# Joint attention: another order of the engines' work in a step, and the query blocks in natural order

## What is computed

```python
def _diff_combine(s, lam):
    p = jax.nn.softmax(s, axis=-1)
    ...
    return p[:, :, 0] - lam * p[:, :, 1]

def diff_attn_prompt(o, q, k, v, lam):      # 8 heads, blocks of 128 queries, causal
    ...
        s = jnp.einsum('bqhd,bkhd->bhqk', qi, k).astype(F32) * HD_C ** -0.5
        s = jnp.where((kpos[None, :] <= qpos[:, None])[None, None], s, -jnp.inf)
        a = _diff_combine(s, lam)
        return jnp.einsum('bhqk,bkhe->bqhe', a, vf)
...
def diff_attn_cached(q, k, v, kp, vp, lam): # 8 samples, 4096 cached keys each, in pages of 128
    s_p = jnp.einsum('bqhd,bkhd->bhqk', q, kp).astype(F32) * scale
    ...
```

## Time and profile before

| what | us |
|---|---|
| three executions | 2852.94, 2854.07, 3822.21 |
| their median | 2854.07 |
| the profiled execution: its own time | 2852.4 |
| its span, first to last instruction | 2850.3 |
| the 64 steps of `attend`, from the first block's scores to the end of the last step's key banks | 1931.9 to 2698.0 |
| busy over the whole span: PE, DVE, ACT | 2569.8, 1363.5, 780.2 |
| bytes moved by DMA | 536.54 MB |

### The profile page before, as it was taken

How to read it: one execution, slowest core, us unless ns; L and a number is a source line. 1 busy time by engine, 2 the same in 40 slices (tenths; PEclk the granted TensorE clock), 3 DMA queues, 4 the chain that set the end, 5 groups by cost and what they waited for, 6 DMA issues and landing times. The chain is left out here.

```text
span 2850.3 us, 46453 instructions
## 1 busy us (share of the span) xinstructions
PE 2569.8 (90%) x16842; PEld 1912.0 (67%) x16842; DVE 1363.5 (48%) x2338; ACT 780.2 (27%) x1978; POOL 416.2 (15%) x240
## 2 busy tenths in 40 slices
PE   6999999999946999499968999969999999999968
PEld 5898889888935777344437888855565566556547
DVE  3656562433242666312223343326766666667643
ACT  3222211111121333111111111114454455545521
POOL 4324321432200000000004232100000000000021
PEclk7999999999976999799989999988999999999979
DMA  4233222322217788732112525159999999999863
GB/s 125 91 105 97 80 84 93 118 71 84 77 41 210 236 269 278 215 146 83 48 55 70 143 84 142 55 160 345 353 384 368 363 359 383 371 354 374 294 203 117
DMA packets 332817, 536.54 MB, mean 188 GB/s; under 512 B 29765, under 2 KB 242130, under 8 KB 329402
## 3 DMA queue, kind: packets, MB, share of 16 engines
q1 hardware_dynamic: 329698, 525.33, 54.2%
q10 hardware_dynamic: 2936, 8.82, 0.8%
HBM read 432.73 MB, written 101.22 MB: 187 GB/s over the span
## 5 line engine op out<-in xcount | busy, mean ns | idle before, releaser
L2355 PE MATMUL at_ring<-ident,at_kp 128*128 128x128 f32 x2048 | 305.2, 281 | 25.3 <-ACT at_kT L2455 9.6
L2355 PEld LDWEIGHTS at_ring<-ident,at_kp 128*128 128x128 f32 x2048 | 225.0, 141 | 149.0 <-issue 117.8
L511 PE MATMUL p_col<-h_hi,p_wqk 128*128 128x352 f32 x768 | 250.5, 326 | 3.3 <-DVEq L713 3.3
L513 PE MATMUL p_col<-h_hi,p_wqk 128*128 128x352 f32 x768 | 246.6, 321 | 0.0
L512 PE MATMUL p_col<-h_lo,p_wqk 128*128 128x352 f32 x768 | 246.3, 321 | 0.0
L1657 PE MATMUL oa_out<-oa_w,oa_yT 128*128 128x512 f32 x512 | 225.8, 599 | 8.5 <-ACT oa_yT L1713 5.4
L2455 ACT ACTIVATE at_kT<-at_ring 128x512 f32<-128x512 f32 x256 | 153.4, 599 | 263.6 <-PE at_ring L2355 263.6
L1954 PE MATMUL p_gm<-p_whl,h_hi 128*128 128x512 f32 x512 | 202.3, 395 | 7.8 <-POOLq L2040 7.8
L2581 DVE COPY at_kT<-at_ring 128x512 f32<-128x512 f32 x256 | 176.9, 691 | 64.7 <-PE at_ring L2355 49.4
L555 PE MATMUL p_row<-p_wvz,h_hi 128*128 128x512 f32 x512 | 203.7, 398 | 3.3 <-ACT p_vst L632 3.3
L557 PE MATMUL p_row<-p_wvz,h_lo 128*128 128x512 f32 x512 | 202.0, 394 | 0.0
(11 more groups left out here) (368 smaller groups left out, 4436.1 us busy)
## 6 DMA issues: line engine op xcount, KB each, us to landing
at_kp<-in_cache_k SPq DMA_DIRECT2D x256, 512.0 KB, 5.9
at_vp<-in_cache_v SPq DMA_DIRECT2D x256, 512.0 KB, 5.9
s_qk<-p_res SPq DMA_DIRECT2D x32, 528.0 KB, 2.8
p_wst<-in_w_in_a SPq DMA_DIRECT2D x32, 512.0 KB, 4.0
p_wst<-in_w_in_a SPq DMA_DIRECT2D x64, 256.0 KB, 3.1
mx_qk<-s_qk SPq DMA_DIRECT2D x16, 1024.0 KB, 10.6
p_wst<-in_w_in_c SPq DMA_DIRECT2D x64, 256.0 KB, 5.6
s_v<-p_vst SPq DMA_DIRECT2D x64, 128.0 KB, 2.8
```

What stands on the lines that cost most here:

```text
L511: pe.matmul(out[:, r, 0:TN], wx[:, 0, k, :], h_hi[:, k, at], start=k == 0, stop=False)
L513: last = pe.matmul(out[:, r, 0:TN], wx[:, 1, k, :], h_hi[:, k, at], start=False, stop=k == KD - 1)
L2355: last = pe.transpose(bank("key", n, f)[:, h * PAGE:(h + 1) * PAGE], kp[:, n % 2, k, tile:tile + P], c.ident[:])
```

## The change

Three things are changed, all inside `attend`.

1. `q_block` returns `s % NB`: blocks 0, 1, 2 ... 7 of a head in this order, not small and large ones in turn.
2. PE's list: key banks 2 and 3 come together, then the first part of the page scores, and only then the weights' transpositions (before: key bank 2, weights, key bank 3, page scores). The ring's order follows it: the weights' banks come after key bank 3.
3. ACT takes key bank 0 ahead of `page_exps`, and key bank 4 ahead of the first exponential of the block. DVE takes one key bank between any two other pieces, `add_page` moves ahead of both maxima, `page_top` behind key bank 5, and `difference` to the end of the step, behind key bank 7.

The instructions of a head and their sizes are the same as before, in another order.

```diff
         def q_block(s):
-            return (0, 7, 1, 6, 2, 5, 3, 4)[s % NB]
+            return s % NB
...
-            for f in range(2 * GP):
-                if keys_at(s_):
-                    use("key", s_, f, ("act", "dve")[f % 2])
-                if f == 1 and values_at(s_):
-                    use("val", s_ - 3, 0, "dve")
-                if f == 2 and weights_at(s_):
...
+            use_keys(s_, 0, 1)
+            if values_at(s_):
+                use("val", s_ - 3, 0, "dve")
+            use_keys(s_, 2, 3)
+            if weights_at(s_):
+                for i in range((tiles(s_ - 1) + 3) // 4):
+                    use("wgt", s_ - 1, i, ("act", "dve")[i])
+            use_keys(s_, 4)
...
@@ PE @@
+                    if later:
+                        turn_keys(s, 2)
+                        turn_keys(s, 3)
+                    if weights_at(s):
+                        page_scores(s - 1, 0)
+                        turn_weights(s - 1)
+                    if later:
+                        turn_keys(s, 4)
+                    if weights_at(s):
+                        page_scores(s - 1, 1)
...
@@ ACT @@
+                    if later:
+                        take_keys(s, 0)
                     if rows_at(s):
                         page_exps(s - 2)
                     if later:
-                        take_keys(s, 0)
                         take_keys(s, 1)
                     if weights_at(s):
                         take_weights(s - 1)
+                    if later:
+                        take_keys(s, 2)
                     if keys_at(s):
                         exps(s, 0)
-                    if later:
-                        take_keys(s, 2)
...
@@ DVE @@
-                    if keys_at(s):
-                        mask_scores(s)
                     if later:
                         take_keys(s, 0)
                     if keys_at(s):
-                        maximum(s, 0)
+                        mask_scores(s)
                     if values_at(s):
                         add_page(s - 3)
+                    if later:
+                        take_keys(s, 1)
+                    if keys_at(s):
+                        maximum(s, 0)
+                    if weights_at(s):
+                        take_weights(s - 1)
                     if keys_at(s):
                         maximum(s, 1)
-                    if weights_at(s):
-                        take_weights(s - 1)
                     if later:
-                        take_keys(s, 1)
+                        take_keys(s, 2)
                     if weights_at(s):
                         page_top(s - 1)
                     if later:
-                        take_keys(s, 2)
+                        take_keys(s, 3)
                     if keys_at(s):
                         difference(s)
-                    if later:
-                        take_keys(s, 3)
```

More of the change, by code:

```diff
@@ L2201, in pick_at, with use_keys @@
             return (s - 4) // NGB if s >= 4 and (s - 4) % NGB == NGB - 1 else None
+        def use_keys(s, *parts):
+            for f in parts:
+                if keys_at(s):
+                    use("key", s, f, ("act", "dve")[f % 2])
         for s_ in range(LAST):
-            for f in range(2 * GP):
-                if keys_at(s_):
-                    use("key", s_, f, ("act", "dve")[f % 2])
-                if f == 1 and values_at(s_):
-                    use("val", s_ - 3, 0, "dve")
-                if f == 2 and weights_at(s_):
[L2210 to L2215, removed]
+            use_keys(s_, 0, 1)
[6 more added lines that the diff above has]
+            use_keys(s_, 4)
+            if rows_at(s_):
+                use("row", s_ - 2, 0, "act")
+            use_keys(s_, 5)
+            if weights_at(s_):
+                use("out", s_ - 1, 0, "act")
+            use_keys(s_, 6, 7)
             if pick_at(s_) is not None:
@@ L2422, in _ @@
                 for s in range(LAST):
[L2423 to L2437, removed]
+                    later = keys_at(s) and s > 0
+                    if later:
+                        turn_keys(s, 0)
+                        turn_keys(s, 1)
+                    if values_at(s):
+                        page_values(s - 3)
+                    if later:
[8 more added lines that the diff above has]
+                        page_scores(s - 1, 1)
+                    if rows_at(s):
+                        turn_rows(s - 2)
+                    if later:
+                        turn_keys(s, 5)
+                    if weights_at(s):
+                        sum_values(s - 1)
+                    if later:
+                        turn_keys(s, 6)
+                        turn_keys(s, 7)
                     if s + 1 < NG:
```

3 lines of the change are left out of this document (added).

## The result

The changed kernel takes 2804.27 us in the median of four executions (2802.64 to 2807.97), the kernel before 2854.43. The ratio is 0.9826, with a 95% interval of 0.9812 to 0.9841. The profiled execution took 2802.64 us, with a span of 2800.1. The execution of 3822.21 us in the table of the kernel before is left out of the comparison.

What follows compares the result with a forecast made beforehand. PE's work was taken as the floor, DMA second. Waits removed less new ones, 30.0 - 4.3 = 25.7 us, + 2.3 + 1.2 - 1.5 = 27.7 off 2852.4 gave 2824.7, or 2826 against the median; range 2812 to 2846.

Steps and rivals of the forecast that it cites:

- the carried lag of the loads: Page loads fall behind by 0.5 us in block 1's step and 4.5 in block 3's; blocks 4 to 7 recover it.
- Rivals 2 and 3: DMA rate can't rise, head stays 97 us, 2854 (chance 0.10); light steps wait for pages, 2866 (chance 0.06).
- rival 1: New waits from DVE's or ACT's order in heavy steps eat about half the gain: 2843 us, chance 0.19.
- The wait behind the hand-over: PE's wait for ACT before the bank behind the hand-over: 1.3 of 1.37 us a head stays.
- The seam behind block 7: Key bank 1's copy behind block 7's difference just meets PE's need for key bank 3: 0.2 us a head.
- The other new wait, 0.4 behind block 1: Block 1's step: difference, scaling and delayed key bank 7 make key bank 1's copy late, 0.4 us a head.
- PE's work is then 91.8 us a head: PE's work taken as the 97.2 us head less 5.4 us of waits.
- the sum stays 91.8: In the natural block order PE's steps run from 9.7 to 13.0 us, with 91.8 us a head unchanged.
- rival 4: All waits gone, the hand-over's too, PE having no more to give: 2813 us, chance 0.05.
- 30.0 - 4.3 in 700: PE's waits removed, 30.0 us, less new waits of the new order, 4.3 us, in 700 us of the stage.
- the two new waits: Seams where key bank 1's copy follows the difference, behind blocks 7 and 1: together 0.6 us a head.
- 15.8 + 5.2 us: Key bank 7 ahead of difference ends waits before the value product (15.8) and key bank 1 (5.2) in 700 us.

Runs made afterwards that it cites:

- e8: The changed kernel with the hand-over's DMA issues on GpSimd, further without the value products of all tiles but the first: 2775.22 us, one execution.
- e2: The changed kernel with the old order of the query blocks put back: 2815.86 us, ratio 0.9871.
- e6: The changed kernel with the weights' transpositions back between key banks 2 and 3, and DVE's copy of them ahead of key bank 3: 2822.99 us.
- e13: e6 with one needless transposition of the fifth tile where a block has five tiles: 2822.04 us, one execution.
- e14: The changed kernel with one needless transposition of the fifth tile where a block has five tiles: 2804.18 us, one execution.
- e1: The kernel before with the natural order of the query blocks alone, all engines' lists unchanged: 2836.14 us, ratio 0.9944.
- e3: The kernel before with one swap on DVE, the copy of key bank 7 ahead of the difference: 2867.47 us, ratio 1.0060.
- e11: The kernel before with DVE's new list alone, its copy of the weights kept ahead of key bank 3: 2845.31 us, ratio 0.9968.
- e5: The changed kernel with the difference again ahead of key bank 7 on DVE: 2814.32 us, ratio 0.9860.
- e7: The changed kernel with ACT's old list, page_exps ahead of key bank 0 and the first exponential ahead of key bank 4: 2809.90 us.

## Why the prediction was wrong

**Right.** PE was the bound and stayed it. The block order's step lengths (9.7 to 13), the carried lag of the loads and the absence of waits for pages came as forecast: landing 14.8 at most, 386 to 390 GB/s for a forecast of 381. Rivals 2 and 3 fell, and rival 1 too, with 0.5 us a head of new waits. By the 358 GB/s of the Trainium skill (page "DMA: Bandwidth & Descriptors", section "Where 436 GB/s comes from") a head would have needed 99.6 us, an estimate from that figure; the trace has 91.0, and e8 87.5 in the mean of six heads. The wait behind the hand-over stayed, at 1.12 for a forecast of 1.3. The seam behind block 7 cost 0.35 for 0.2. The other new wait, 0.4 behind block 1, did not come; that step has a gap of 0.12 and no mark.

**Wrong: "PE's work is then 91.8 us a head" and "the sum stays 91.8".** This is the step that failed, and with it rival 4's "PE has no more to give". I took the length of a head less the marked idle time for PE's work. In fact 1.7 us of it were unmarked waits: without what shows in PE's rows a head is 91.5 us before and 89.8 after, and e2 with the old blocks has the same 89.8. One such wait is shown, by e6, e13 and e14: key bank 3 behind ACT's copy of key bank 2 when the weights fill two banks. The old ring can have it in the four steps of eight with more than four tiles of weights, the shorter the more tiles there are. Another is in e1's trace, in the step of block 7, where the weights' second bank waits for add_page; the weight loads' row has 0.33 us there, and PE's row none:

```profile
2195.46 0.47 DVE L2599 SCALAR_TENSOR_TENSOR at_acc<-at_acc,at_alpha,at_ring 128x256 f32<-128x256 f32 x1
2196.05 0.31 PEld L2333 LDWEIGHTS at_ring<-ident,at_pr 128*128 128x128 f32 x3 [0.33 <-DVEq L2601]
```

The trace of the kernel before shows both kinds, in the weight loads' rows of the head from 2124.90 us:

```profile
2130.89 0.42 PEld L2355 LDWEIGHTS at_ring<-ident,at_kp 128*128 128x128 f32 x4 [0.66 <-DVEq L2601]
2143.47 0.42 PEld L2333 LDWEIGHTS at_ring<-ident,at_pr 128*128 128x128 f32 x4 [0.85 <-DVEq L2601]
2181.86 0.42 PEld L2355 LDWEIGHTS at_ring<-ident,at_kp 128*128 128x128 f32 x4 [0.17 <-DVEq L2601]
2193.32 0.42 PEld L2355 LDWEIGHTS at_ring<-ident,at_kp 128*128 128x128 f32 x4 [0.27 <-ACT at_kT L2455]
2215.91 0.42 PEld L2355 LDWEIGHTS at_ring<-ident,at_kp 128*128 128x128 f32 x4 [0.38 <-ACT at_kT L2455]
```

PE's rows have 0.42, 0.62, 0, 0.03 and 0.14 at these places, so a marked wait too is longer by 0.23 or 0.24 than its mark. I add up the whole head in this way; where the kind of product changes, I first take off the idle time that the weight loads have there in every step, wait or not (0.17 before a value product, 0.41 behind one). It gives 7.5 us of waits, of which PE's rows show 5.6. The hidden 1.9 are 0.9 of waits for add_page, 0.6 of key bank 3 waiting for ACT's copy, and 0.4 on other copies. The changed kernel has 1.5 us of waits in the same count and hides 0.4, nearly all of it in the seam behind block 7. So the count has 6.0 of the 6.2 us a head, and 1.5 of the 1.7 that were hidden; for the remaining 0.2 I have no row.

**Mis-sized: the marked waits.** The list over 700 us gave 5.4 a head, and so do the marks in the steps; with the gaps too short for a mark it is 5.7. Of these 4.5 went (5.7 to 1.24), where the account had 30.0 - 4.3 in 700, some 3.5 a head. Of the difference, 0.3 are those gaps, 0.2 the wait behind the hand-over (1.12 for 1.3), and 0.5 the two new waits (0.12 in PE's rows for 0.6). Together with the 1.7 that is 6.2 us a head for 3.5: 19 of the 22 us that the forecast is off. The rest lies outside the 700 us, 5.8 us for the 2.0 that I gave to the start and the end of the stage: 50.2 us in all, less 7.2 x 6.16. I did not take it apart.

**Wrong in the parts: the waits don't belong to one edit each.** The account gave 15.8 + 5.2 us to key bank 7's place. Alone (e3) that edit made the kernel 14 us slower: the wait moved to key bank 1 and did not shrink, and the clock fell in eight steps, which is some 10 of the 14. DVE's whole list alone (e11) brings 8 us, the block order 17 (e1), each with the clock falling in some steps; the lists of all three engines and the ring bring 37 (e2), all together 50. Taken back one at a time from the changed kernel, the weights' place costs 19 us (e6), key bank 7's 10 (e5), ACT's list 6 (e7). I had given the weights' place no term of its own.

## What to carry to other kernels

With a ring of few buffers, write down for each copy out the filling that is its deadline, and move the copies and the fillings together; a single late copy that is moved ahead hands its wait to the next one, as e3 shows. Don't take "length less marked idle time" for an engine's work: compare the distance of equal pieces in steps of different load, and read the weight loads' waits beside PE's, since gaps of a few tenths of a microsecond show there alone. And when PE's waits are gone, look at what a queue of an engine holds up (four DMA issues on ACT were 1.2 us a head), and move it to an idle one.

## What the runs showed of the hardware that I had not expected

- A wait of some 2 us on PE can cost more than itself. In e1, after an idle stretch of 2.23 us, the granted clock stood at 0.50 and then 0.66 in windows of 2 us, and the step was 1.6 us longer. Behind the seven hand-overs of a trace that happened seven times in e3 (waits of 1.97 to 2.44 us), four times in e1 (1.97 to 2.23), three times in e11 (1.99 to 2.11), and never in e7 (1.97 to 2.10) or in the changed kernel (1.12 to 1.26). In e1 one wait of 1.97 us cost 1.6 more (15.17 us for the step) and another of 1.97 nothing (13.54), so the length of the wait alone doesn't decide it; what does stays open.
- PE's group of five and PE's group of six transpositions took the same 0.85 us up to the next piece in e6 (for 0.60 and 0.71 in steps without a wait), both without a mark: the distance to the next piece holds a wait that no mark gives, and the weight loads' row has it (0.38 and 0.27 us).
- One core's 16 DMA engines gave 407 to 409 GB/s over six whole heads of e8, with pages of 512 KB, at a median landing of 13.2 us; at the changed kernel's 394 it was 7.0. While the buffers lasted, PE used pages faster than that (415 GB/s over three heads).
